# Router fed with unnormed rows, weight loads and bias products re-ordered, and the overflow table built between two item loops

## The chip, the cores and the metric

The kernel runs on one core of one Trainium2 chip. The metric is device time in microseconds (us). Five engines work side by side and meet at semaphores: TensorE (PE, matmuls), VectorE (DVE), ScalarE (ACT), GpSimd (POOL) and SyncE (SP, which here only issues transfers). Each runs its own list of instructions strictly in order.

## The reference, cut to what matters

One layer on 512 rows of 1024 values: a mixing block (gated linear attention and stick-breaking attention), a cross attention over 256 memory rows, and a mixture of experts, all in float32. The change touches only the last part.

```
h = rmsnorm(x, g_ffn)                       # x * rsqrt(mean(x*x)+eps) * g
logits = h @ w_router + b_router            # 32 experts
top 4 of 32 per row, gates = softmax(top values)
for each expert e, its rows in blocks:
    gu = xb @ w_gu[e] + b_gu[e]             # gate half, lin half (1024 each)
    act = (clip(lin)+1) * gate*sigmoid(1.702*gate)
    y = act @ w_down[e] + b_down[e]         # weighted by the gate, added to the row
y = rmsnorm(x + moe)
```

## The kernel before

The expert part works through **items**. An item is up to 96 rows of one expert, with the 8 MB of `w_gu` and 4 MB of `w_down` of that expert. Items 0 to 31 are the first 96 rows of each expert; further items would hold rows past 96 (**overflow**). The input here has none: 32 items run. Each item's weights come in 12 loads of 1 MiB ("chunks" 0 to 3 of `lin`, `gate` and `down`), issued by SP in a fixed order; a chunk's place in `ring` is loaded again once PE has multiplied it. `lin` and `down` weights are split on the chip: ACT makes the rounded part (`w_hi_a`, `w_hi_x`), DVE the remainder (`ring_split`), and PE multiplies three products.

PE's work on item t stands in two functions. `lin_and_gate(t)` multiplies the `lin` chunks (L1026) interleaved with the first half of the gate (L1007); `down_and_gate(t)` multiplies `down` (L1051) with the second half of the gate. In the steady loop PE alternates `down_and_gate(t)` and `lin_and_gate(t + 1)`. Item 0 and the start of item 1 are written out ahead of the loop, since they differ: item 0's second gate half (32 blocks) runs alone.

Ahead of the items stands the **router**, in the order that the list `ROUTE` gives PE: `y2` (the last eight pieces of the cross attention's output projection, L625), `h3` (transposes of a tile of 128 rows), `lg` (logits), `rk` (ranks of the picks within their expert), `tb` (the item table: which row stands in which slot). DVE takes the results in an order of its own (`choose`, `rank`, `weigh`, `sum_gates`); ACT norms the rows. POOL then gathers an item's 96 rows from `rows_scratch` in HBM (L2219) and later adds the results to `acc_scratch` with a scatter. `acc_scratch` starts as x plus the gated sum of `b_down`: eight **bias products** (`bd`, L981) whose results DVE adds to `X` (L1971), which is then stored.

`overflow()` on DVE (L1915 to L1956) counts further items, publishes their number (`s_items`), and prepares the overflow table. PE multiplies that in 16 matmuls (L1082), and `overflow_out()` copies it out. All of this stands between item 0 and item 1.

```
lin_transpose(0)
pe.wait_ge(s_xnext, 2)
pe.wait_ge(s_over, 1)
for n in range(16):
    last = mm(psum[0:C, Y0, 0:3 * MORE], lhsT=over_slot[:, n, :], ...)
lin_and_gate(1)
```

Of the kernel before, what the change touches and what calls it, by code (L numbers as in the profile page):

```python
# [33 lines left out]
P = 128  # L34
# [18 lines left out]
PADS = C  # L53
LIMIT = 7.0
# [5 lines left out]
class Banks:  # L60
# [41 lines left out]
]  # L102


def plan_banks():
# [48 lines left out]
    plan.add(("count",), "dve", pool=most)  # L154
    plan.add(("gatesT",), "dve", pool=most)
    for i in range(TT):
        for half in range(2):
            plan.add(("bd", i, half), "dve", pool=most)
# [8 lines left out]
def build(nc, x, mem, g_mix, w_in, w_gla_gate, b_gla_gate, g_gla_head, w_out, g_mem_q, g_mem_kv,  # L167
# [5 lines left out]
    with ExitStack() as ctx:  # L173
# [98 lines left out]
        gate_eT = VGb[:, 768:896]  # L272
        bdown = VSb[:, 1024:2048]

        MORE = MAX_ITEMS - E
        earlier_e = VGb[:, 1024:2048].rearrange("p (a b) -> p a b", a=E)
# [10 lines left out]
        oh_over = VSb[:, 0:512].rearrange("p (n e) -> p n e", n=16)  # L287
# [253 lines left out]
        def _(sp):  # L541
# [25 lines left out]
            for c in range(4):  # L567
                wait_filled(sp, SLOT_FREED[2 + c // 2])
                load_gate(0, c)
            for c in range(4):  # L570
                wait_filled(sp, SLOT_FREED[c // 2])
                load_down(0, c)
            for c in range(4):
                sp.wait_ge(s_lused, c + 1)
                load_lin(1, c)
            for c in range(4):
# [31 lines left out]
        def _(pe):  # L608
# [310 lines left out]
            def route_transpose(i):  # L919
                pe.wait_ge(s_xn, 2 * TT + i + 1)  # L920
                for u in range(2):
                    b = begin(("h3", i, u))
                    for k in range(4):
                        last = nc.tensor.transpose(b[:, k * P:(k + 1) * P],
                                                   xn[:, i, (4 * u + k) * P:(4 * u + k + 1) * P], ident[:, :])
# [21 lines left out]
            def route_table(i):  # L947
                b = begin(("table",)) if i == 0 else bank(("table",))
                pe.wait_ge(s_onehot, i + 1)
                for k in range(K):  # L950
                    last = mm(b[0:C, 0:3 * E], lhsT=in_slot[i][:, k, :], rhs=pick_rhs[:, K * i + k, :],
                              start=i == 0 and k == 0, stop=i == TT - 1 and k == K - 1)
                if i == TT - 1:
                    done(last)

# [17 lines left out]
            pe.wait_ge(s_gatee, TT)  # L973
            b = begin(("gatesT",))
            done(nc.tensor.transpose(b[:, 0:P], gate_e.rearrange("p i e -> p (i e)"), ident[:, :]))
            wait_emptied(pe, ("gatesT",))
            pe.wait_ge(s_bd, 64)
            for i in range(TT):
                for half in range(2):
                    b = begin(("bd", i, half))  # L980
                    done(mm(b, lhsT=gate_eT[i * E:(i + 1) * E, :],  # L981
                            rhs=bdown[i * E:(i + 1) * E, half * 512:(half + 1) * 512],
                            start=True, stop=True))

            wait_emptied(pe, ("bd", 3, 1))
# [11 lines left out]
            def lin_transpose(t):  # L997
# [13 lines left out]
            def lin_and_gate(t):  # L1011


                pe.wait_ge(s_xlo, t + 1)
# [3 lines left out]
                for c in range(4):  # L1018
                    pe.wait_ge(s_llo, 4 * t + c + 1)
                    for pos in range(12):  # L1020
# [4 lines left out]
                        cols_ = (lin_lo(c) if b else chunk_hi(c))[:, k2, half * 512:half * 512 + 512]  # L1025
# [9 lines left out]
                    if c == 2 and isinstance(t, int) and t == 0:  # L1035
# [23 lines left out]
            def down_and_gate(t, transpose_next=True):  # L1059
# [3 lines left out]
                for c in range(4):  # L1063
                    down_chunk(t, c, True)
                    if c == 0:
                        lin_transpose(t)
# [4 lines left out]
            pe.sem_inc(s_dused, 4)  # L1071
            item_transpose(0)
            lin_and_gate(0)
            for c in range(4):
# [5 lines left out]
            pe.wait_ge(s_over, 1)  # L1080
# [1204 lines left out]
```

## Time and profile before

| | |
|---|---|
| median of 3 runs | 1723.5 us (1723.45 to 1723.79) |
| the profiled execution, its own time | 1721.68 us |
| its span in the trace | 1719.9 us |
| PE busy | 1646.6 us, 96% |
| DVE, ACT, POOL busy | 63%, 48%, 8% |
| items, from 585.0 us on | 31 periods of about 36.1 us |

The profiled execution lies 1.8 us below the median and its span another 1.8 us below its own time. Times below are places in the span. "idle before" is the time that an engine stood still ahead of an instruction, with what ended it.

### The profile page before, as it was taken

How to read it: one execution, taken by the hardware profiler on the slowest of the kernel's cores; microseconds unless marked ns; L12 is line 12 of the kernel's file. 1: busy time of each engine (PE TensorE's matmuls, PEld its weight loads, DVE VectorE, ACT ScalarE, POOL GpSimd, SP SyncE). 2: the span in 40 equal slices, each digit the busy share in tenths (PEclk: the TensorE clock that was granted, in tenths of full speed). 3: DMA queues.
4: the chain of work that ended last, by engine and by line, in shares of the span. 5: the costliest groups of instructions: out<-in, count | busy, mean ns of one | idle time of the engine just before them, and what ended most of it. 6: DMA issues, size and time to landing. Idle time of an engine off the chain costs nothing.

```text
span 1719.9 us, 26975 instructions
## 1 busy us (share of the span) xinstructions
PE 1646.6 (96%) x10074; PEld 1380.3 (80%) x10074; DVE 1080.7 (63%) x1173; ACT 831.6 (48%) x844; POOL 132.3 (8%) x217
## 2 busy tenths in 40 slices
PE   7999989999988899999999999999999999999994
PEld 5876657987776788888888888888888888888883
DVE  4221554433357777777777777776777767777774
ACT  4243363533322446555555555555454554546553
POOL 0020220000000001000000000010000100001000
PEclk9999989999988999999999999999999999999997
DMA  5111123322049799999999999999999999999993
GB/s 204 49 50 50 49 99 122 124 89 99 16 143 396 259 375 366 377 362 374 362 382 364 376 365 363 378 375 370 368 361 382 368 370 373 362 374 370 377 338 116
DMA packets 134870, 477.09 MB, mean 277 GB/s; under 512 B 10337, under 2 KB 10386, under 8 KB 134802
## 3 DMA queue, kind: packets, MB, share of 16 engines
q1 hardware_dynamic: 123968, 446.72, 69.4%
q0 software_dynamic: 7168, 25.17, 6.2%
q10 hardware_dynamic: 3698, 4.70, 0.8%
q8 instruction: 25, 0.41, 0.1%
q14 instruction: 11, 0.09, 0.0%
HBM read 457.69 MB, written 18.87 MB: 277 GB/s over the span
## 4 chain that ended last, share of the span: by engine, by line
PE 90%; DVE 4%; ACT 3%; DMA 2%; issue 1%; ACTq 0%; POOL 0%; SPq 0%; DVEq 0%; POOLq 0%
PE psum L1007 22%; PE psum L1051 21%; PE psum L1026 20%; PE psum L625 17%; PE psum L804 1%; PE psum L793 1%; PE psum L1001 1%; PE psum L993 1%; PE psum L781 1%; PE psum L896 1%; PE psum L916 1%; DMA acc_scratch<-X 1%; ACT ring_split L1151 1%; DVE ring_split L1996 1%; PE psum L935 1%
## 5 line engine op out<-in xcount | busy, mean ns | idle before, releaser
L1007 PEld LDWEIGHTS psum<-MIX,ring 128*128 128x128 f32 x4096 | 776.1, 191 | 101.7 <-DVE MIX L2035 1.6
L1007 PE MATMUL psum<-MIX,ring 128*128 128x96 f32 x4096 | 726.5, 260 | 0.9 <-DVE MIX L2035 0.9
L1996 DVE TENSOR_TENSOR ring_split<-ring,w_hi_a 128x2048 fp32r<-128x2048 f32 x64 | 146.4, 2288 | 86.8 <-ACT w_hi_a L1417 86.4
L1026 PE MATMUL psum<-ring_split,xs_hi 128*96 128x512 f32 x512 | 200.3, 437 | 0.0
L1051 PE MATMUL psum<-ring_split,act_hi 128*96 128x512 f32 x512 | 198.1, 434 | 0.0
L2008 DVE TENSOR_TENSOR ring_split<-ring,w_hi_x 128x2048 fp32r<-128x2048 f32 x62 | 141.8, 2287 | 84.8 <-ACT w_hi_x L1428 84.8
L1996 DVE TENSOR_TENSOR ring_split<-ring,w_hi_x 128x2048 fp32r<-128x2048 f32 x64 | 146.4, 2289 | 77.5 <-ACT w_hi_x L1417 77.5
L625 PE MATMUL psum<-ring_split,H_hi 128*128 128x512 f32 (+1 forms) x512 | 151.8, 380 | 0.6 <-DVE ring L1646 0.6
L2008 DVE TENSOR_TENSOR ring_split<-ring,w_hi_a 128x2048 fp32r<-128x2048 f32 x62 | 141.6, 2284 | 2.2 <-ACT w_hi_a L1428 2.2
L1417 ACT ACTIVATE w_hi_x<-ring 128x2048 fp32r<-128x2048 f32 x64 | 121.3, 1897 | 7.3 <-DMA acc_scratch<-X 7.3
L1417 ACT ACTIVATE w_hi_a<-ring 128x2048 fp32r<-128x2048 f32 x62 | 117.7, 1899 | 12.6 <-DMA ring<-in_w_gu 12.6
L1439 ACT ACTIVATE MIX<-MIX 128x384 f32<-128x384 f32 x64 | 33.1, 517 | 182.0 <-DVE MIX L2052 182.0
L1428 ACT ACTIVATE w_hi_a<-ring 128x2048 fp32r<-128x2048 f32 x62 | 118.0, 1903 | 3.4 <-PE psum L1026 3.4
L1026 PE MATMUL psum<-w_hi_a,xs_hi 128*96 128x512 f32 x256 | 110.9, 445 | 8.0 <-DVE xs_lo L2029 8.0
L1445 ACT ACTIVATE xs_hi<-MIX 128x768 fp32r<-128x768 f32 x32 | 27.0, 845 | 188.3 <-DVE MIX L2023 188.3
L1428 ACT ACTIVATE w_hi_x<-ring 128x2048 fp32r<-128x2048 f32 x62 | 118.0, 1904 | 0.0
L1051 PE MATMUL psum<-w_hi_a,act_hi 128*96 128x512 f32 x256 | 110.0, 443 | 0.0
L1051 PE MATMUL psum<-w_hi_x,act_hi 128*96 128x512 f32 x256 | 109.5, 442 | 0.0
L1026 PE MATMUL psum<-w_hi_x,xs_hi 128*96 128x512 f32 x256 | 109.4, 439 | 0.0
L625 PEld LDWEIGHTS psum<-ring_split,H_hi 128*128 128x128 f32 x512 | 93.0, 188 | 19.1 <-DVE ring L1646 0.8
L1434 ACT ACTIVATE H<-psum 96x1024 f32<-96x1024 f32 x32 | 32.6, 1019 | 138.3 <-PE psum L1026 138.3
L1026 PE MATMUL psum<-w_hi_a,xs_lo 128*96 128x512 f32 x256 | 97.0, 425 | 0.0
(305 smaller groups left out, 2674.8 us busy)
## 6 DMA issues: line engine op xcount, KB each, us to landing
ring<-in_w_gu SPq DMA_DIRECT2D x256, 1024.0 KB, 10.3
ring<-in_w_down SPq DMA_DIRECT2D x128, 1024.0 KB, 12.1
ring<-in_w_in SPq DMA_DIRECT2D x6, 2048.0 KB, 10.1
X<-in_x SPq DMA_DIRECT2D x8, 512.0 KB, 7.6
ring<-in_w_out SPq DMA_DIRECT2D x2, 2048.0 KB, 7.8
ring<-in_w_mk SPq DMA_DIRECT2D x2, 2048.0 KB, 9.1
ring<-in_w_mv SPq DMA_DIRECT2D x2, 2048.0 KB, 7.8
ring<-in_w_mq SPq DMA_DIRECT2D x2, 2048.0 KB, 8.7
```

What stands on the lines that cost most here:

```text
L625: ins = mm(dst, lhsT=lhs(a, k), rhs=rhs(b, k), start=n == 0 and j == 0, stop=n == KT - 1 and j == 2)
L781: last = mm(sb_seg(h, i), lhsT=ksT[r:r + 64, j, i * P:(i + 1) * P], rhs=qsT[r:r + 64, j, i * P:T], start=SB_SEG[i][1] == 0, stop=True, ski ...
L1007: return mm(psum[:, dst, q * C:(q + 1) * C], lhsT=gate_w(k // 2)[:, k % 2, f * P:(f + 1) * P], rhs=xsT[:, k, :], start=k == 0 and q == 0, ...
L1026: x_last = mm(psum[0:C, L0 + half, :], lhsT=rows_, rhs=cols_, start=k == 0 and n == 0, stop=k == KT - 1 and n == 2, skip_group_check=True)
L1051: x_last = mm(psum[0:C, to + half, :], lhsT=rows_, rhs=cols_, start=f == 0 and n == 0, stop=f == KT - 1 and n == 2, skip_group_check=True)
L1417: go(chunk_hi(c), lin_w(c), ACT.Copy).then_inc(s_lhi, 1)
L1428: go(chunk_hi(c), down_w(c), ACT.Copy).then_inc(s_dhi, 1)
L1434: go(lin_rows.rearrange("p (a b) -> p a b", a=2), psum[0:C, 2:4, :], ACT.Copy)\
L1439: go(sig_h, gate_h, ACT.Sigmoid, scale=ALPHA).then_inc(s_sig, 1)
L1445: go(xs_hi[:, :, :], xs_next, ACT.Copy).then_inc(s_xhi, 1)
L1996: v.tensor_tensor(lin_lo(c), lin_w(c), chunk_hi(c).bitcast(F32), ALU.subtract)\
L2008: v.tensor_tensor(down_lo(c), down_w(c), chunk_hi(c).bitcast(F32), ALU.subtract)\
```

## The change

- **Router.** PE transposes `X` itself and not the normed rows; the scale `rstd` is applied to the logits when DVE takes them. ACT computes `rstd` first (`rstd_3`) and the normed rows after it (`rows_3`). `ROUTE` and DVE's order are changed.
- **Table.** The item table holds rows only; its gates come from 16 matmuls of their own (`route_gates`, bank `tgate`), after the counts.
- **Loads.** Item 0's `lin` chunks are issued ahead of the row stores, and two of its `gate` chunks ahead of the last of these. `down` chunks 2 and 3 of item 0 wait for the first gather; 0 and 1 stand behind `lin` chunks 2 and 3 of item 1, since their place now holds the rounded part of item 0's `lin` chunks 2 and 3 (`first_hi`). The stores to `acc_scratch` go from ACT's queue to SP's, between `lin` chunks 1 and 2 of item 1.
- **Bias products.** Five of eight stand ahead of `lin_and_gate(0)`, three inside it. `item_transpose(0)` no longer waits for them.
- **Overflow.** `overflow()` keeps the count of items, with a shorter running sum. The rest is `overflow_rows()`; it, PE's 16 matmuls and `overflow_out()` stand behind the item loop's passes 1 and 2. The loop is now two loops, 1 to 2 and 3 to m. POOL gathers items 1 to 5 before it waits for the table.

```diff
+            for i in range(TT):
+                if i == TT - 1:
+                    for c in range(2):
+                        wait_filled(sp, SLOT_FREED[2 + c // 2])
+                        load_gate(0, c)
...
+                sp.wait_ge(s_xn, 2 * TT + i + 1)
+                sp.dma_start(rows_dram[i * P:(i + 1) * P, :], xn[:, i, :]).then_inc(s_rowsout, 16)
...
             def route_transpose(i):
-                pe.wait_ge(s_xn, 2 * TT + i + 1)
+                pe.wait_ge(s_res, TT + i + 1)
...
-            wait_emptied(pe, ("bd", 3, 1))
...
+            wait_emptied(pe, ("tgate",))
             item_transpose(0)
+            wait_emptied(pe, ("gatesT",))
+            pe.wait_ge(s_bd, 64)
+            for piece in BD[0:3]:
+                add_bias(piece)
+            pe.wait_ge(s_xnext, 1)
+            for piece in BD[3:5]:
+                add_bias(piece)
             lin_and_gate(0)
...
-            with pe.Fori(1, m) as t:
+            with pe.Fori(1, TABLE_AT) as t:
+                down_and_gate(t, after_table=False)
+                lin_and_gate(t + 1)
+            pe.wait_ge(s_over, 1)
+            for n in range(16):
+                last = mm(psum[0:C, T0, 0:3 * MORE], lhsT=over_slot[:, n, :], rhs=over_rhs[:, n, :],
+                          start=n == 0, stop=n == 15)
+            last.then_inc(s_overt, 1)
+            with pe.Fori(TABLE_AT, m) as t:
                 down_and_gate(t)
                 lin_and_gate(t + 1)
...
+            with dve.Fori(1, TABLE_AT) as t:
+                item(t)
+            overflow_rows()
+            overflow_out()
+            with dve.Fori(TABLE_AT, m) as t:
+                item(t)
```

SP's list, from the row stores to item 1's gate loads, before (L556 is `load_lin`, L559 `load_gate`, L562 `load_down`):

```order
L554 DMA rows_scratch<-A 128x1024 [waits normed_rows_ready] x4
L556 DMA ring<-in_w_gu 128x2x1024 [waits psum_bank_filled] x4
L559 DMA ring<-in_w_gu 128x2x1024 [waits psum_bank_filled] x4
L562 DMA ring<-in_w_down 128x2x1024 [waits psum_bank_filled] x4
L556 DMA ring<-in_w_gu 128x2x1024 [waits lin_chunk_multiplied] x4
L559 DMA ring<-in_w_gu 128x2x1024 [waits gate_chunk_multiplied] x4
```

The same stretch after the change (L565 is `load_lin`, L568 `load_gate`, L571 `load_down`):

```order
L565 DMA ring<-in_w_gu 128x2x1024 [waits psum_bank_filled] x4
L585 DMA rows_scratch<-A 128x1024 [waits normed_rows_ready] x3
L568 DMA ring<-in_w_gu 128x2x1024 [waits psum_bank_filled] x2
...
L585 DMA rows_scratch<-A 128x1024 [waits normed_rows_ready]
L568 DMA ring<-in_w_gu 128x2x1024 [waits psum_bank_filled] x2
...
L565 DMA ring<-in_w_gu 128x2x1024 [waits lin_chunk_multiplied] x2
L598 DMA acc_scratch<-X 128x1024 [waits residual_with_bias_ready] x4
L565 DMA ring<-in_w_gu 128x2x1024 [waits lin_chunk_multiplied]
L571 DMA ring<-in_w_down 128x2x1024
L565 DMA ring<-in_w_gu 128x2x1024 [waits lin_chunk_multiplied]
L571 DMA ring<-in_w_down 128x2x1024
L568 DMA ring<-in_w_gu 128x2x1024 [waits gate_chunk_multiplied] x4
```

Four stores and two `down` loads now stand between item 1's `lin` loads, and all of them ahead of its `gate` loads.

PE's list around the overflow table after the change (the last rows of the first loop, the 16 matmuls, the head of the second loop):

```order
L1062 MATMUL psum<-w_hi_x,xs_lo 96x512 x2
L1132 REGISTER_ALU
L1132 COMPARE_AND_BRANCH
L1137 MATMUL psum<-MIX,RGb 96x63 [waits overflow_onehots_ready]
L1137 MATMUL psum<-MIX,RGb 96x63 x15
L1140 UNCONDITIONAL_BRANCH
L1140 ISA
L1082 ISA [waits gate_half_clamped]
L1084 REGISTER_ALU [waits down_chunk_lo_ready]
L1091 MATMUL psum<-w_hi_a,act_hi 96x512 [waits act_half_lo_ready]
```

Before, the 16 matmuls (L1082) stood right behind `lin_transpose(0)` and ahead of `lin_and_gate(1)`.

DVE's list at the same place after the change (the end of an item's pass, then `overflow_rows`):

```order
L2077 TENSOR_TENSOR ring_split<-ring,w_hi_a 128x2048 [waits down_chunk_hi_ready]
L2204 REGISTER_ALU
L2204 COMPARE_AND_BRANCH
L1997 TENSOR_SCALAR QGb<-QGb 128x16
L1999 SCALAR_TENSOR_TENSOR QGb<-QGb 128x16 [waits dve_step] x4
...
L2019 TENSOR_TENSOR RGb<-KDb,QGb 128x1536
L1947 TENSOR_SCALAR KDb<-psum,QGb 96x21 [waits overflow_table_filled]
```

The vector work that PE's 16 matmuls wait for now begins only after DVE's last instruction of the pass for item 2.

## Rows read from the trace of the kernel before

**Rows 1.** The page: span, and the chain that ended last.

```profile
span 1719.9 us, 26975 instructions
PE 90%; DVE 4%; ACT 3%; DMA 2%; issue 1%; ACTq 0%; POOL 0%; SPq 0%; DVEq 0%; POOLq 0%
```

**Rows 2.** Windows: start:end, length, busy by engine, granted PE clock, DMA share, GB/s.

```profile
512.00:519.00 7.00, 5.14 (x17) 1.94 (x17) 2.86 (x11) 1.63 (x1) 1.14 (x1) 0.54 1.04 400
529.00:533.00 4.00, 4.00 (x16) 3.52 (x16) 2.25 (x2) 0.00 (x0) 0.00 (x0) 0.50 1.03 411
533.00:556.00 23.00, 23.00 (x171) 20.74 (x169) 18.31 (x42) 8.55 (x6) 0.92 (x1) 1.00 1.03 397
564.00:571.00 7.00, 6.14 (x25) 5.16 (x24) 6.52 (x14) 2.85 (x3) 0.00 (x0) 0.53 0.38 152
571.00:585.00 14.00, 14.00 (x91) 11.86 (x91) 8.26 (x9) 4.24 (x3) 0.00 (x0) 1.00 0.64 200
585.00:621.00 36.00, 36.00 (x241) 31.04 (x240) 26.56 (x26) 19.39 (x16) 2.71 (x3) 1.00 0.99 338
```

**Rows 3.** Timeline of PE, router to item 0: start, length, idle before.

```profile
502.33 3.56 PE L935 MATMUL psum<-QGb,RGb 128*128 128x32 f32 x16 [0.71 <-DVE RGb L1803]
...
514.33 4.92 PE L981 MATMUL psum<-VSb,VGb 32*128 32x512 f32 x16 [0.38 <-DVE VGb L1911]
523.30 1.51 PE L993 MATMUL psum<-ident,H 96*128 96x96 f32 x8 [4.05 <-DVE X L1971]
528.63 0.74 PE L1026 MATMUL psum<-w_hi_a,xs_hi 128*96 128x512 f32 x1 [3.82 <-DVE xs_lo L2029]
```

**Rows 4.** Timeline of DVE: router, head of item 0.

```profile
501.50 0.68 DVE L1803 COPY RGb<-psum 128x512 f32<-128x512 f32 x1
...
523.48 2.29 DVE L1996 TENSOR_TENSOR ring_split<-ring,w_hi_a 128x2048 fp32r<-128x2048 f32 x1 [0.33 <-DVE X L1971]
525.69 1.02 DVE L2023 TENSOR_TENSOR MIX<-psum,gcols 128x384 f32<-128x384 f32 x2
```

**Rows 5.** POOL's gathers: issue of the first, and its time to landing.

```profile
513.45 1.14 POOL L2219 DMA_INDIRECT H<-rows_scratch,KDb  x1 [58.73 <-DVEq L1904]
...
DMA to landing us min/median/max: 8.4/8.4/8.4
```

**Rows 6.** Timeline of PE, items 0 to 2.

```profile
539.52 0.40 PE L1026 MATMUL psum<-w_hi_x,xs_hi 128*96 128x512 f32 x1
...
548.87 7.28 PE L1007 MATMUL psum<-MIX,ring 128*128 128x96 f32 x64
555.98 0.85 PE L1001 MATMUL psum<-ident,H 96*128 96x96 f32 x8
556.67 2.85 PE L1082 MATMUL psum<-MIX,RGb 128*96 128x63 f32 x32
563.70 0.67 PE L1026 MATMUL psum<-w_hi_a,xs_hi 128*96 128x512 f32 x1 [4.18 <-DVE xs_lo L2029]
565.23 0.74 PE L1007 MATMUL psum<-MIX,ring 128*128 128x96 f32 x2 [0.86 <-DVE MIX L2035]
...
576.30 0.40 PE L1026 MATMUL psum<-w_hi_x,xs_hi 128*96 128x512 f32 x1
...
585.00 0.40 PE L1051 MATMUL psum<-w_hi_a,act_hi 128*96 128x512 f32 x1
...
621.11 0.40 PE L1051 MATMUL psum<-w_hi_a,act_hi 128*96 128x512 f32 x1
```

**Rows 7.** DMA issues from 571 to 586 us: size, us from issue to landing.

```profile
ring<-in_w_gu SPq DMA_DIRECT2D x4, 1024.0 KB, 5.4
```

**Rows 8.** Timeline of DVE: the overflow work, and the end of an item's pass.

```profile
548.03 0.17 DVE L1934 TENSOR_SCALAR QGb<-QGb 128x16 f32<-128x16 f32 x1
...
552.97 1.75 DVE L1956 TENSOR_TENSOR RGb<-KDb,QGb 128x1536 f32<-128x1536 f32 x1
...
617.14 2.28 DVE L2008 TENSOR_TENSOR ring_split<-ring,w_hi_a 128x2048 fp32r<-128x2048 f32 x1
```

More of the change, by code:

```diff
@@ L53 @@
 PADS = C
+TABLE_AT = 3
 LIMIT = 7.0
@@ L98 @@
 ROUTE = [
[3 rows of a table removed]
-]
[3 rows of a table added]
+]
+BD = [(i, half) for half in range(2) for i in range(TT)]
+BD_BANK = dict(zip(BD, (1, 6, 7, 4, 5, 1, 4, 5)))
 def plan_banks():
@@ L153, in plan_banks @@
     plan.add(("table",), "dve", pool=(7,))
[L154 to L158, printed above, removed]
+    plan.add(("count",), "dve", pool=(0,))
+    plan.add(("tgate",), "dve", pool=(3,))
+    plan.add(("gatesT",), "dve", pool=(2,))
+    for i, half in BD:
+        plan.add(("bd", i, half), "dve", pool=(BD_BANK[i, half],))
     return plan
@@ L954, in route_table, with route_gates @@
                     done(last)
+            def route_gates():
+                b = begin(("tgate",))
+                for i in range(TT):
+                    pe.wait_ge(s_gatee, i + 1)
+                    for k in range(K):
+                        last = mm(b[0:C, 0:E], lhsT=in_slot[i][:, k, :], rhs=pick_rhs[:, K * i + k, 2 * E:3 * E],
+                                  start=i == 0 and k == 0, stop=i == TT - 1 and k == K - 1)
+                done(last)
             for step in ROUTE:
@@ L972, in _, with add_bias @@
             done(mm(b[:, 0:E], lhsT=ones[:, :], rhs=picks_upto[:, TT - 1, :], start=True, stop=True))
-            pe.wait_ge(s_gatee, TT)
+            route_gates()
             b = begin(("gatesT",))
             done(nc.tensor.transpose(b[:, 0:P], gate_e.rearrange("p i e -> p (i e)"), ident[:, :]))
[L976 to L983, printed above, removed]
-            wait_emptied(pe, ("bd", 3, 1))
+            def add_bias(piece):
+                i, half = piece
+                b = begin(("bd", i, half))
+                done(mm(b, lhsT=gate_eT[i * E:(i + 1) * E, :],
+                        rhs=bdown[i * E:(i + 1) * E, half * 512:(half + 1) * 512], start=True, stop=True))
             G0, G1, L0, T0, Y0 = 0, 1, 2, 4, 6
@@ L1011, in lin_and_gate @@
             def lin_and_gate(t):
+                first = isinstance(t, int) and t == 0
                 pe.wait_ge(s_xlo, t + 1)
@@ L1079, in _ @@
             pe.wait_ge(s_xnext, 2)
-            pe.wait_ge(s_over, 1)
-            for n in range(16):
-                last = mm(psum[0:C, Y0, 0:3 * MORE], lhsT=over_slot[:, n, :], rhs=over_rhs[:, n, :],
-                          start=n == 0, stop=n == 15)
-            last.then_inc(s_overt, 1)
             lin_and_gate(1)
@@ L1873, in _ @@
             sum_gates(0)
+            add_residual("y2", 2, 1)
+            choose(1)
+            rank(0)
             add_residual("y2", 3, 0)
             h3_out(2)
-            choose(1)
-            rank(0)
             weigh(1)
@@ L2080, in _ @@
             xT_next(0)
+            add_bias(BD[0])
             xT_lo(0)
@@ L2107, in _, with item @@
             st.finish()
-            with dve.Fori(1, m) as t:
+            def item(t):
                 st = Steps(t)
```

206 lines of the change are left out of this document (121 added, 85 removed), and 6 rows, old and new, of the table ROUTE.

## The prediction, made before the result was known

> **What bounds the kernel now.** I read the page first: 90% of the chain that ended last is PE [rows 1]. So time is won only where PE stands still, runs at the lower clock, or does work that can go. The windows by stage say where that is. From 585 us on PE is busy in all of the stretch at a granted clock of 1.00 [rows 2], and an item takes 621.11 - 585.00 = 36.1 us of PE work [rows 6]. Both kernels run the same 31 such periods, so the comparison is settled by the moment at which `down_and_gate(1)` starts (585.0 before), plus whatever is put in behind it. PE's timeline ahead of that shows the waits: 4.05 us and 3.82 us around the first item's transposes [rows 3], and 4.18 us and 0.86 us ahead of item 1 [rows 6]. The windows add the clock: 0.50 to 0.54 (the lower of its two levels, 1.2 of 2.4 GHz) from 512 to 533 and again from 564 to 571 [rows 2]. Last I read the transfers: from 512 to 564 they run without a break at 397 to 411 GB/s [rows 2].
>
> **Router.** It should save nothing. PE transposes the last tile earlier, since it no longer waits for the normed rows. But the logits' matmuls began at 502.33, released by DVE's copy at 501.50 [rows 3, 4], and in DVE's new order that copy still stands behind `choose(2)` and `rank(1)`. What is won is small: `rk` of the last tile stands ahead of one `tb`, and the gates leave the table. I put the first gather's issue 0.5 us earlier, from 513.45 to 513.0 [rows 5].
>
> **Item 0 starts earlier.** Before, the gather landed 8.4 us after its issue [rows 5] with the transfers at 400 GB/s [rows 2], and PE then waited for the bias sums until 523.30 [rows 3]. After, `lin` and most `gate` loads are over and the `down` loads wait for the gather, so it meets idle engines. Its 0.39 MB (96 rows of 4 KB) at 400 GB/s take 1 us; no row shows an unloaded gather. I estimate 6.4 us (bounds 5.5 and 8.4), so 519.4. Transposes at the lower clock take 1.5 us [rows 3]: 520.9. From `xT_next` to the first matmul took 528.63 - 525.69 = 2.94 us [rows 3, 4], and the one bias sum put between fits ScalarE's time there. Start: **523.8** (522.3 to 525.8) against 528.63, 4.8 us won. The matmuls for `tgate` (32 passes, half of them ahead of the last gates) and DVE's first 2.29 us subtraction fill the wait for the gather; if they come last instead, they cost up to the upper bound.
>
> **Item 0 itself.** From its start to the end of chunk 1 was 539.52 - 528.63 = 10.9 us, while two chunks take 585.00 - 576.30 = 8.7 us at full clock [rows 6], so the lower clock cost 2.2. PE is busier ahead of item 0 now, so I charge half of that: chunk 1 ends at 523.8 + 8.7 + 1.1 = 533.6 (531.0 to 536.7). Three bias products inside the item add about 0.9 us (eight took 4.92 at the lower clock [rows 3], 0.31 each at full). The item to the end of `lin_transpose(0)` was 556.67 - 528.63 = 28.0 us [rows 3, 6]; now 28.0 + 0.9 - 1.1 = 27.8, ending at 551.6. Were nothing else in the way, PE would begin item 1 there.
>
> **What is late next: item 1's gate weights.** A gate chunk's place is free only when item 0's separate second gate half has used it, so this load cannot be early. SP's new list puts ahead of it, all issued from the end of chunk 1 on: `lin` 1, four stores (2 MiB), `lin` 2, `down` 0, `lin` 3, `down` 1. With the gate chunk that is 8 MiB; `g_final`'s 0.5 MiB and one gather (0.4) share the engines: 8.9 MiB. The last issue before it comes less than 11 us after the first, so the queue never drains. At the 405 GB/s of the windows [rows 2] a MiB takes 2.6 us. A single load met idle engines in 5.4 us [rows 7]. So `gate` 0 lands at 533.6 + 5.4 + 7.9 x 2.6 = **559.5**, and PE, which after its first matmul needs it at 551.9, stands for 7.6 us. Bounds: 24 us (8.9 MiB at the highest rate shown, 411 GB/s, and little more than a start of a microsecond) to 26.5 us after the end of chunk 1, so 555.0 to 563.2. The other three gate chunks follow at 2.6 us and PE uses one in 4.35, so they do not delay it.
>
> The Trainium skill, "DMA: Bandwidth & Descriptors", section Bandwidth, gives about 358 GB/s as what HBM grants one core and lets that side bind loads. By that a MiB takes 2.93 us and PE would wait 2.9 us longer. The windows here stand at 397 to 411 for 50 us, so the measurement decides, and the page's figure is left a small chance.
>
> **Item 1.** Before, from 563.70 to 585.00 = 21.3 us: 17.4 at full clock (twice 8.7), 0.86 of waiting, 3.0 for the clock, which was 0.53 behind 4.18 us of standing still [rows 2, 6]. After 7.6 us of standing still it will be low again. A stretch at the lower clock cost 2.2 and 3.0 us in these two places; I take 2.6 (1.8 to 3.4). `down_and_gate(1)` starts at 559.5 + 17.1 + 2.6 = **579.2**, against 585.0: 5.8 us won.
>
> **The table is now paid for.** Before, DVE's overflow work (548.03 to 554.72 = 6.7 us [rows 8]) lay under item 0's gate blocks, and PE's 2.85 us of matmuls lay in a gap that ended at 563.70 anyway [rows 6]: together they cost nothing. After, `overflow_rows` starts when DVE ends its pass, at 617.14 + 2.28 = 619.4 in a period that PE ends at 621.1 [rows 6, 8], 1.7 us ahead of PE. It takes 6.7 us, so PE stands 5.0 us. Then come the 2.85 us of matmuls, and the lower clock again, since 4.18 us of standing still were enough for it: 2.6. Sum **10.4 us** (9.6 to 11.3). DVE has slack in the next item (26.6 busy of 36 [rows 2]) and `overflow_out` (six instructions on at most 96 x 21 values) lies under `down` chunk 0, so nothing further is late. POOL's wait for the table stands behind five gathers and holds up nothing.
>
> **Sum.** -5.8 + 10.4 = +4.6 us. The profiled execution would go from 1721.7 to 1726.3 us of its own time; the median is 1.8 above that, so **1728.1 us**. At the bounds: start 522.3, chunk 1 at full clock, 24 us and 1.8 give 573.9, and with 9.6 a sum of -1.5; the other end gives 583.7 and with 11.3 a sum of +10.0.
>
> **Rivals.**
> - *The gate chunk is there in time* (faster). Place: PE's second instruction of item 1. PE would start item 1 at 551.6, keep the full clock, and reach `down_and_gate(1)` at 569.0: 16.0 won, 10.4 paid, **-5.6 us, 1717.9**. For it: loads are issued so early that the queue stands empty before the end of chunk 1. Against: 8.9 MiB need over 22 us at the rate of any window shown, and PE leaves 18. It decides the sign once gate 0 lands before about 555. Chance 0.15.
> - *DVE's table work is hidden*. If DVE ran ahead of PE by 7 us in passes 1 and 2, only 2.85 us would be paid: -3.0 us, **1720.5**. For it: DVE is idle 9 us in each item [rows 2]. Against: that idle time lies inside the pass, in waits for ScalarE and PE; its last instruction ends 1.7 us ahead of PE [rows 6, 8]. Chance 0.12.
> - *Item 0 is no earlier*. If gate matmuls, the subtraction and the gather's fixed time come one after another, the start stays at 528.6 and all behind it moves 4.8 us: +9.4, **1732.9**. Against: the 4.05 us wait for the bias sums is surely gone [rows 3]. Chance 0.12.
> - *The slower transfer rate*: +7.5, **1731.0**. Chance 0.05.
> - That the router part does nothing is already in the sum; were it to bring the logits forward by the 3 us of the norming, the result would be 1725.
>
> **How the numbers follow.** A difference of 0.2% (3.4 us) is about what a measurement of this kernel can tell from no change. The forecast has 0.56, with a range of its own of 1722 to 1733; some 0.7 of it lies above 1727. Slower: 0.56 x 0.7 + 0.12 + 0.05, less a little for what I overlook on the good side, 0.53. Faster: the first rival and a part of the second, 0.18. Within 0.2%: 0.29. The range goes from the first rival to the third, 1718 to 1733.
>
> **What would show it.** Right: in the changed trace PE's first matmul of item 0 near 523.8; a PE wait of 6 to 9 us at the first gate matmul of item 1, ended by a load of `w_gu`, with a clock near 0.5 behind it; one wait of about 5 us ahead of the 16 table matmuls two periods later, ended by DVE's `over_slot`, again with the lower clock; then periods of 36.1 us to the end. Wrong: no wait for that load; DVE done with the table when PE comes; a clock that stays at 1.00 over either wait (2.6 us less each); or a first matmul later than 526.

## The result and the profile after

The changed kernel is slower: 1730.35 us median of 5 runs (1729.2 to 1732.91) against 1723.5 us of before (1723.04 to 1723.86) on the same chip. The recorded ratio of the runs is 1.0046, with a 95% interval of 1.0035 to 1.0058 (the quotient of the two medians is 1.0040). The profiled execution took 1730.79 us of its own time.

The page of the changed kernel, its span, its chain and its costliest group:

```profile
span 1729.0 us, 27040 instructions
...
PE 91%; ACT 3%; DVE 3%; DMA 2%; issue 1%; ACTq 0%; POOL 0%; SPq 0%; DVEq 0%; POOLq 0%
...
L1041 PE MATMUL psum<-MIX,ring 128*128 128x96 f32 x4096 | 727.1, 260 | 10.1 <-DMA ring<-in_w_gu 10.1
```

The chain reads like that of before [rows 1], though PE's gate matmuls now have 10.1 us of idle time ahead of them, all for one load. PE's waits in the changed kernel, from the router to item 4 (engine, line, releaser: us in total, times, longest us):

```profile
PE psum L1041 <- DMA ring<-in_w_gu: 10.1, 1, 10.1
PE psum L1137 <- DVE RGb L2019: 4.8, 1, 4.8
PE psum L962 <- DVE RGb L1856: 1.9, 1, 1.9
PE psum L1025 <- DMA H<-rows_scratch,KDb: 0.6, 1, 0.6
```

The waits around item 0 are gone (4.05 and 3.82 us in [rows 3]). Two have come: 10.1 us for item 1's gate weights and 4.8 us for the overflow table. The windows of the changed kernel (columns as in [rows 2]):

```profile
512.00:519.00 7.00, 6.40 (x40) 6.13 (x39) 3.95 (x17) 5.21 (x3) 1.14 (x1) 0.50 0.27 78
529.00:533.00 4.00, 4.00 (x27) 3.39 (x26) 3.84 (x3) 0.00 (x0) 0.00 (x0) 1.00 0.23 51
...
535.00:537.00 2.00, 2.00 (x13) 1.08 (x13) 0.69 (x1) 0.00 (x0) 0.00 (x0) 1.00 0.63 143
537.00:545.00 8.00, 8.00 (x59) 7.02 (x58) 6.65 (x25) 3.83 (x2) 0.92 (x1) 1.00 0.99 351
545.00:556.00 11.00, 8.78 (x77) 8.27 (x75) 8.18 (x10) 4.19 (x4) 0.00 (x0) 1.00 1.03 368
556.00:564.00 8.00, 0.11 (x1) 0.14 (x1) 7.27 (x10) 2.85 (x3) 0.00 (x0) 0.50 1.02 412
564.00:571.00 7.00, 7.00 (x28) 6.00 (x29) 1.82 (x3) 0.00 (x0) 0.00 (x0) 0.60 0.80 320
...
630.00:666.00 36.00, 31.17 (x201) 27.13 (x200) 25.03 (x36) 17.15 (x14) 2.74 (x3) 0.89 0.91 337
666.00:690.00 24.00, 24.00 (x158) 20.82 (x158) 18.38 (x24) 9.00 (x7) 1.13 (x2) 0.95 0.73 220
```

In the first two of these windows, around item 0's start, the transfers nearly rest now (78 and 51 GB/s, where [rows 2] have 400 and 411). From 556 to 564 the queues are full, at 412 GB/s, while PE does nothing and its clock falls to the lower level. PE's own rows in the changed kernel:

```profile
504.15 3.01 PE L962 MATMUL psum<-QGb,RGb 128*128 128x32 f32 x16 [1.86 <-DVE RGb L1856]
...
518.86 1.51 PE L1025 MATMUL psum<-ident,H 96*128 96x96 f32 x8 [0.60 <-DMA H<-rows_scratch,KDb]
520.30 3.77 PE L1016 MATMUL psum<-H,STb 32*128 32x512 f32 x10
524.01 0.74 PE L1062 MATMUL psum<-w_hi_a,xs_hi 128*96 128x512 f32 x1
...
563.89 0.71 PE L1041 MATMUL psum<-MIX,ring 128*128 128x96 f32 x2 [10.12 <-DMA ring<-in_w_gu]
...
583.81 0.40 PE L1091 MATMUL psum<-w_hi_a,act_hi 128*96 128x512 f32 x1
...
661.02 5.38 PE L1137 MATMUL psum<-MIX,RGb 128*96 128x63 f32 x32 [4.83 <-DVE RGb L2019]
666.16 0.72 PE L1091 MATMUL psum<-w_hi_a,act_hi 128*96 128x512 f32 x1
```

Item 0 starts at 524.01 (before 528.63), item 1's gate at 563.89, `down_and_gate(1)` at 583.81 (before 585.00 [rows 6]). The last row but one is the table: PE stood 4.83 us, and its matmuls took 5.38 us instead of 2.85 [rows 6].

**Where the difference arose.** Work ahead of the router's last matmuls takes a different time in each execution, by up to 5 us. So I cut each trace in two: from the start of the logits of tile 2 (the "anchor": 496.23 before, 497.99 after) to `down_and_gate(1)`, and from there to the end of the span.

| kernel | anchor to `down_and_gate(1)` | from there to the end |
|---|---|---|
| before | 88.8 | 1134.9 |
| changed | 85.8 | 1145.2 |
| changed, a second trace | 84.1 | 1146.3 |

The head won 3.0 us (4.7 in the second trace), the rest lost 10.3 (11.4).

### The profile page after: what moved, and what is told of

The parts are those of the page before. It is cut to its first block, busy times and chain, and to the rows that moved or that the text cites. A ratio compares the mean times of both kernels' runs of the same rounds, so it can differ in the third digit from the quotient of the medians.

```text
span 1729.0 us, 27040 instructions
## 1 busy us (share of the span) xinstructions
PE 1656.2 (96%) x10106; PEld 1389.4 (80%) x10106; DVE 1079.8 (62%) x1178; ACT 831.5 (48%) x844; POOL 129.3 (7%) x213
## 4 chain that ended last, share of the span: by engine, by line
PE 91%; ACT 3%; DVE 3%; DMA 2%; issue 1%; ACTq 0%; POOL 0%; SPq 0%; DVEq 0%; POOLq 0%
PE psum L1041 23%; PE psum L1091 21%; PE psum L1062 20%; PE psum L652 17%; PE psum L831 1%; PE psum L1025 1%; PE psum L820 1%; PE psum L1035 1%; PE psum L808 1%; DMA ring<-in_w_gu 1%; PE psum L923 1%; PE psum L943 1%; ACT ring_split L1203 1%; PE psum L962 0%; DVE ring_split L1613 0%
## 5 line engine op out<-in xcount | busy, mean ns | idle before, releaser
L1041 PEld LDWEIGHTS psum<-MIX,ring 128*128 128x128 f32 x4096 | 777.1, 191 | 110.9 <-issue 10.4
L1041 PE MATMUL psum<-MIX,ring 128*128 128x96 f32 x4096 | 727.1, 260 | 10.1 <-DMA ring<-in_w_gu 10.1
L2077 DVE TENSOR_TENSOR ring_split<-ring,w_hi_x 128x2048 fp32r<-128x2048 f32 x62 | 141.8, 2288 | 82.1 <-ACT w_hi_x L1481 82.1
L2065 DVE TENSOR_TENSOR ring_split<-ring,w_hi_x 128x2048 fp32r<-128x2048 f32 x62 | 141.9, 2289 | 71.8 <-ACT w_hi_x L1470 71.8
L1470 ACT ACTIVATE w_hi_x<-ring 128x2048 fp32r<-128x2048 f32 x62 | 117.6, 1897 | 3.7 <-DMA ring<-in_w_gu 3.7
L1481 ACT ACTIVATE w_hi_x<-ring 128x2048 fp32r<-128x2048 f32 x62 | 118.0, 1903 | 0.0
L1062 PE MATMUL psum<-w_hi_x,xs_hi 128*96 128x512 f32 x248 | 105.9, 439 | 0.0
```

The lines of the kernel that those rows point to most:

```text
L1041: return mm(psum[:, dst, q * C:(q + 1) * C], lhsT=gate_w(k // 2)[:, k % 2, f * P:(f + 1) * P], rhs=xsT[:, k, :], start=k == 0 and q == 0, ...
L1062: x_last = mm(psum[0:C, L0 + half, :], lhsT=rows_, rhs=cols_, start=k == 0 and n == 0, stop=k == KT - 1 and n == 2, skip_group_check=True)
L1470: go(chunk_hi(c), lin_w(c), ACT.Copy).then_inc(s_lhi, 1)
L1481: go(chunk_hi(c), down_w(c), ACT.Copy).then_inc(s_dhi, 1)
L2065: v.tensor_tensor(lin_lo(c), lin_w(c), hi.bitcast(F32), ALU.subtract)\
L2077: v.tensor_tensor(down_lo(c), down_w(c), chunk_hi(c).bitcast(F32), ALU.subtract)\
```

## The experiments

The first four ran on one chip (before there: 1721.24 us), the next four on a second (1722.61), the last three on a third (1722.16). Ratios are to the runs of before on the same chip.

**1. The table back between items 0 and 1.** The first loop runs from 1 to m again, on PE and DVE; all else stays as changed.

```diff
             pe.wait_ge(s_xnext, 2)
+            pe.wait_ge(s_over, 1)
+            for n in range(16):
+                last = mm(psum[0:C, Y0, 0:3 * MORE], lhsT=over_slot[:, n, :], ...)
             lin_and_gate(1)
```

> The changed kernel with one thing undone: the overflow rows, the 16 table matmuls and the copy out stand between items 0 and 1 again, and the item loop is one loop. Theory (two new waits): in the changed kernel the table costs 11.3 us (4.8 us of PE standing still, 5.4 us of matmuls at the lower clock, the rest the lower clock behind them), and here it falls into PE's 10.1 us wait for item 1's gate weights, so it costs nothing: about 1719 us against 1730.4 for the changed kernel and 1723.5 for before. Rival 1 (the table costs its matmuls only, the loss lies elsewhere): 1727.5 us. Rival 2 (the overflow work delays item 1's rows on VectorE past the landing of the gate weights): 1721 us or more, with a PE wait on xs_lo or on the one-hots ahead of item 1.

Measured: 1719.39 us, ratio 0.9991 (0.998 to 1.0002). PE in this kernel, around the table:

```profile
556.21 4.29 PE L1131 MATMUL psum<-MIX,RGb 128*96 128x63 f32 x32 [1.46 <-DVE RGb L2016]
...
564.58 0.71 PE L1041 MATMUL psum<-MIX,ring 128*128 128x96 f32 x2 [3.60 <-DMA ring<-in_w_gu]
```

The wait for the gate chunk is 3.6 us where it was 10.1, though the chunk lands at the same distance from the anchor (65.5 us; 65.9 in the changed kernel). The table work lies in time in which PE would have stood anyway. The rest behind `down_and_gate(1)` is 1134.6 us, as before. So the whole loss, and more, is the table's. A little of rival 2 is there, a wait of 1.46 us for the one-hots, but it lies ahead of a gate chunk that PE would have waited for anyway.

**2. Item 1's gate chunks ahead of item 0's `down` chunks 0 and 1**, the table still behind item 2.

```diff
             for c in range(2, 4):
                 sp.wait_ge(s_lused, c + 1)
                 load_lin(1, c)
-                load_down(0, c - 2)
             for c in range(4):
                 sp.wait_ge(s_gused, c + 1)
                 load_gate(1, c)
+            for c in range(2):
+                load_down(0, c)
```

> The changed kernel with SP's list altered in one place: item 0's down chunks 0 and 1 are issued behind item 1's four gate loads instead of ahead of them. Theory (PE waits for gate chunk 0 because 8.9 MiB stand ahead of it in the queue): 2 MiB less ahead of it, so it lands 5 us earlier, PE's wait of 10.1 us shrinks to about 5, and the time is about 1725.3 us. Rival 1 (the wait has another cause than the queue, such as the issue time): still 10 us, 1730.4 us. Rival 2 (the two down chunks are then late for item 1): a new PE wait ahead of the down products, 1728 us or more.

Measured: 1725.44 us, ratio 1.0023 (1.0014 to 1.0033). PE's first gate matmul of item 1 in this kernel:

```profile
557.59 0.71 PE L1042 MATMUL psum<-MIX,ring 128*128 128x96 f32 x2 [4.95 <-DMA ring<-in_w_gu]
```

That is 60.7 us behind the anchor, 5.2 us earlier than in the changed kernel (65.9 and 65.4 in its two traces, 66.5 in experiment 7, which is the same up to there): about what two loads of 1 MiB take at 2.6 us. PE's wait halves, and `down_and_gate(1)` comes 5.9 us sooner than in the first trace of the changed kernel and 4.2 sooner than in the second.

**3. `overflow_rows()` on DVE during item 0**, with only `overflow_out()` and PE's matmuls left between the loops.

```diff
             lin_lo_part(1, 0)
+            overflow_rows()
...
-            overflow_rows()
             overflow_out()
             with dve.Fori(TABLE_AT, m) as t:
```

> The changed kernel with VectorE's overflow_rows (6.7 us) moved back between items 0 and 1; PE's 16 matmuls and the copy out stay behind item 2, between the two loops. Theory (the table is dear because PE stands still for VectorE and the clock falls): no PE wait ahead of the 16 matmuls, they run at the full clock in 2.9 us, and the table costs 3 us in place of 11.3: about 1722 us. Rival (the narrow matmuls themselves or the loop's border bring the clock down, or cost the time): 5.4 us of matmuls at the lower clock again, 1726 us or more.

Measured: 1722.74 us, ratio 1.001 (1.0 to 1.002). PE's table matmuls in this kernel have no wait and run at full clock:

```profile
659.08 2.85 PE L1137 MATMUL psum<-MIX,RGb 128*96 128x63 f32 x32
```

The rest behind `down_and_gate(1)` is 1137.2 us, 2.3 above before, against 10.3 above in the changed kernel. So 8.0 us hang on the wait, of which it is itself only 4.8.

**4. PE's transpose of the router waits for the normed rows again**, and ACT writes those first.

```diff
-                pe.wait_ge(s_res, TT + i + 1)
+                pe.wait_ge(s_xn, 2 * TT + i + 1)
```

> The changed kernel, but PE's router transposes wait for the normed rows as before (the rows that they read stay the unnormed ones; ScalarE norms the last tile ahead of its copy). Theory (the last tile's logits wait for VectorE's copy, which stands behind choose(2) and rank(1), not for the transposes): no difference, 1730.4 us within 1 us. Rival (unnormed rows bring the logits forward by the norming): 2 to 3 us slower than the changed kernel, about 1733 us.

Measured: 1731.32 us, ratio 1.0063 (1.0049 to 1.0077), on another chip than the pair of the result. PE's transposes of the last tile in this kernel:

```profile
499.99 1.97 PE L951 MATMUL psum<-ident,X 128*128 128x128 f32 x8 [1.61 <-ACT A L1427]
```

The recorded theory (no difference, since DVE's copy holds the logits) fell in its place: the wait is back, and the last tile's logits start 7.7 us behind the anchor, 6.2 in the changed kernel and 6.1 before. Item 0 starts 2.2 us later in the trace, and since PE then waits for the same gate chunk, `down_and_gate(1)` comes only 0.8 us later. So the unnormed rows do carry 1.6 to 2 us in the new order, and the new order of the stages takes as much away: the router as a whole delivers its logits no sooner than before.

**5. Edits 1 and 2 together.**

> The two repairs of e1 and e2 together: the table between items 0 and 1, and item 0's down chunks 0 and 1 behind item 1's gate loads. Theory: in e1 PE ended the table's matmuls 61.4 us behind the start of the last logits-but-one and waited 3.6 us more for gate chunk 0; in e2 that chunk landed 60.7 us behind the same point. So no wait for it is left, PE starts item 1 when the table's matmuls end, and the kernel is 3 to 4.5 us faster than e1: a ratio of about 0.9970 to before (1718.5 us against 1723.5). Rival (VectorE's chain is next, since the table now delays the rows of item 1 and lin chunk 1 of item 1): equal to e1 within 1 us, with PE waits on xs_lo or on ring_split inside item 1.

Measured: 1712.99 us, ratio 0.9945 (0.9931 to 0.9959). It beats both kernels. PE's waits in it, from 506 to 800 us:

```profile
PE psum L1132 <- DVE RGb L2017: 1.5, 1, 1.5
PE psum L1026 <- DMA H<-rows_scratch,KDb: 0.6, 1, 0.6
PE psum L973 <- DVE QGb L1876: 0.2, 1, 0.2
```

More was won than the expected 0.9970. Against the changed kernel the table below accounts for most of it: the head is 4.7 us shorter (80.3 against a mean of 85.0) and the rest 11.4, together 16.1 of the 17.9 us between the medians of this chip. Against experiment 1 the heads differ by 3.8 us, as expected; the ratios differ by more (0.9991 for experiment 1, on another chip), and no trace shows why. There is no wait for a weight any more. The table's 1.5 us of waiting and 4.3 us of matmuls lie where PE stood 4.95 us in experiment 2, so they are all but free there (the head is 80.3 against 79.9), and nothing is left to pay behind `down_and_gate(1)` (1134.7 us). The clock still falls, after only 1.5 us of standing still:

```profile
556.00:571.00 15.00, 15.00 (x91) 13.40 (x91) 13.94 (x23) 6.82 (x6) 0.00 (x0) 0.77 1.03 412
```

PE is busy in all of these 15 us at 0.77 of the clock: at most 3.4 us of time still lie here.

**6. Before, with only the table moved** (behind item 2, two loops, POOL's gathers 1 to 5 first); loads, router and bias products as before.

```diff
-            with pe.Fori(1, m) as t:
+            with pe.Fori(1, TABLE_AT) as t:
+                down_and_gate(t, after_table=False)
+                lin_and_gate(t + 1)
+            pe.wait_ge(s_over, 1)
...
+            with pe.Fori(TABLE_AT, m) as t:
```

> The kernel before with one part of the change alone: the overflow rows, the 16 matmuls and the copy out behind item 2, between two loops (the old count, router, loads and bias products stay). Theory: the table costs 11.3 us there, and 3 to 4.5 us come back since VectorE has item 1's rows ready 6.7 us sooner and PE then waits for the gate chunk: 7 to 8.5 us slower than before, a ratio of 1.0045. Rival 1 (the table's place costs nothing, it was the other parts): ratio 1.000 or below. Rival 2 (nothing comes back): 11.3 us, a ratio of 1.0065.

Measured: 1730.91 us, ratio 1.005 (1.0036 to 1.0063). PE in this kernel:

```profile
563.56 0.71 PE L1030 MATMUL psum<-w_hi_a,xs_hi 128*96 128x512 f32 x1 [4.15 <-DVE xs_lo L2039]
...
661.68 5.24 PE L1092 MATMUL psum<-MIX,RGb 128*96 128x63 f32 x32 [4.82 <-DVE RGb L1966]
```

The cost shows without the rest of the change: the same 4.8 us wait, the same slow matmuls, and 1145.6 us behind `down_and_gate(1)`. The total is as expected (8.3 us by the medians), but what came back is 2.8 us for the 3 to 4.5 expected, and not for the reason given: PE waits for `xs_lo`, not for the gate chunk. From item 0's first matmul to item 1's is 32.3 us (563.56 - 531.29), where it was 35.1 before (563.70 - 528.63). So the table work between items 0 and 1 cost before 2.8 us. The rows of DVE show whose: first those of before, then those of this kernel.

```profile
555.57 4.48 DVE L1996 TENSOR_TENSOR ring_split<-ring,w_hi_a 128x2048 fp32r<-128x2048 f32 x2
562.69 0.96 DVE L2029 TENSOR_TENSOR xs_lo<-MIX,xs_hi 128x768 fp32r<-128x768 f32 x1
...
553.39 2.29 DVE L2006 TENSOR_TENSOR ring_split<-ring,w_hi_a 128x2048 fp32r<-128x2048 f32 x1 [1.09 <-ACT w_hi_a L1424]
557.58 2.29 DVE L2006 TENSOR_TENSOR ring_split<-ring,w_hi_a 128x2048 fp32r<-128x2048 f32 x1 [1.90 <-ACT w_hi_a L1424]
562.50 0.96 DVE L2039 TENSOR_TENSOR xs_lo<-MIX,xs_hi 128x768 fp32r<-128x768 f32 x1
```

Before, DVE comes from the overflow rows and works without a gap up to `xs_lo`. Here it stands still for ScalarE's rounding, and its second subtraction (the remainder of `lin` 1) ends 28.6 us behind item 0's first matmul (559.87 - 531.29) where it ended after 31.4 (560.05 - 528.63); `xs_lo` follows 3.6 us later in both. So the 2.8 us are DVE's. PE's 2.85 us of matmuls, nearly the same number, ended at 559.5, 4.18 us ahead of `xs_lo`, and lay inside the wait.

**7. The table one item earlier** (`TABLE_AT = 2`).

```diff
-TABLE_AT = 3
+TABLE_AT = 2
```

> The changed kernel with the border between the two loops behind item 1 in place of item 2 (one number). Theory: VectorE ends every pass 1.7 us ahead of PE, so the table costs the same 11 us wherever in the items it stands: equal to the changed kernel within 1.5 us, with a PE wait of 4.8 us ahead of the 16 matmuls one period earlier. Rival (behind item 1 VectorE is further behind or ahead of PE, since item 1 began with the long wait for its gate weights): a PE wait of a different length, and 3 us or more of difference.

Measured: 1732.13 us, ratio 1.0056 (1.0042 to 1.007). PE around the table in this kernel:

```profile
623.76 5.38 PE L1137 MATMUL psum<-MIX,RGb 128*96 128x63 f32 x32 [4.83 <-DVE RGb L2019]
```

The same wait to the hundredth, one period earlier. The cost belongs to DVE's place behind its pass, not to the particular item.

**8. The changed kernel once more**, unaltered, beside the last three.

> The changed kernel once more, unaltered, on the chip of this group, for its spread and for a second profile. Expected: a ratio of 1.0046 within 0.001; from the last row of the cross attention's output to the start of item 0 26.0 us, PE's wait for gate chunk 0 of item 1 10.1 us, for the one-hots 4.8 us; what differs from the first profile lies ahead of that, in code that the change does not touch.

Measured: 1730.94 us, ratio 1.005 (1.0036 to 1.0064). The waits in its trace are 9.7 us and 4.8 us at the same two lines, and item 0 starts 25.6 us behind the anchor.

**9. The four stores behind item 1's gate chunk 0** instead of between its `lin` chunks 1 and 2.

```diff
-            for i in range(TT):
-                sp.wait_ge(s_x2b, i + 1)
-                sp.dma_start(acc_dram[i * P:(i + 1) * P, :], X[:, i, :])...
...
             for c in range(4):
                 sp.wait_ge(s_gused, c + 1)
                 load_gate(1, c)
+                if c == 0:
+                    for i in range(TT):
+                        sp.wait_ge(s_x2b, i + 1)
+                        sp.dma_start(acc_dram[i * P:(i + 1) * P, :], X[:, i, :])...
```

> The changed kernel with the four stores to acc_scratch behind item 1's gate chunk 0 instead of between its lin chunks 1 and 2. In the changed kernel that gate chunk landed 28.7 us after the issue of lin chunk 1 (563.9 - 535.2). If the whole stretch simply runs at one lower rate (8.9 MiB in 28.7 us less 5.4 is 2.95 us per MiB), taking 2 MiB out brings the chunk 5.9 us forward, to 22.8 us. If the transfers run at 405 GB/s but for the stores, which leave the engines partly idle and slow, it comes forward by 7 to 8 us and is then held by the issues alone (lin 2 at 5.5 us, 5 MiB from there: 21.4 us), and the window behind the stores' old place stands at 395 to 411 GB/s instead of 368. ScalarE waits for the stores ahead of its third rounding of item 1's lin chunks, so PE will stand still there instead, in both theories: the span says nothing, the landing does.

One run, 1729.9 us. PE's first gate matmul of item 1 came 63.4 us behind the anchor, 2.5 us earlier than in the changed kernel's first trace and 2.0 earlier than in its second. Its row, and then the windows of the same kernel:

```profile
561.13 0.71 PE L1042 MATMUL psum<-MIX,ring 128*128 128x96 f32 x2 [7.66 <-DMA ring<-in_w_gu]
```

```profile
537.00:545.00 8.00, 8.00 (x57) 6.98 (x56) 6.71 (x26) 3.33 (x2) 0.92 (x1) 1.00 0.84 258
545.00:556.00 11.00, 8.47 (x75) 8.05 (x73) 8.20 (x11) 2.28 (x3) 0.00 (x0) 1.00 1.01 349
```

Both expectations fell. In this one trace the stores cost the chunk 2 to 2.5 us, less than the 5.9 of an even rate and far less than 7 to 8. Without them the stretch runs slower, 258 GB/s where it was 351, since SP waits for PE to free the next `lin` place and the engines have little queued. And the later stretch stands at 349, not at 395 or more: the stores are not what keeps the rate below 400 there.

**10. Edits 2 and 3 together**, the table's matmuls still behind item 2, and **11. experiment 5 again** on the same chip.

> The changed kernel with both remedies that leave the table at the third item: item 1's gate chunks issued ahead of item 0's down chunks 0 and 1, and overflow_rows on DVE during item 0. Theory (wait of PE for each, additive): the table then costs 2.5 us of matmuls alone as in the kernel with early rows, and the rest behind down_and_gate(1) is 1137.2 us; down_and_gate(1) starts 80 to 81 us behind the anchor unless DVE, now with 6.7 us more work under item 0, releases item 1's low part late (it did so in the kernel with early rows, by 3.4 us, which lay under the longer wait for the gate chunk). With that wait in the open: 82 us, a time 4.5 us below before, ratio 0.9975. Rival: the table's place does not matter once DVE is ahead, and this kernel equals the one with the table back at item 1 and the gates first (0.9945).

> The kernel with the table back between items 0 and 1 and the gate chunks first, unaltered, beside the previous one on the same chip: 0.993 to 0.996 again if its gain is real.

Measured: 1716.74 us, ratio 0.9972 (0.9962 to 0.9983), and 1713.46 us, ratio 0.9956 (0.9943 to 0.997). PE's waits in the first of the two, from 506 us on:

```profile
PE psum L1063 <- DVE xs_lo L2099: 3.3, 1, 3.3
PE psum L1042 <- DMA ring<-in_w_gu: 0.8, 1, 0.8
```

The wait for item 1's low part is in the open, as expected, since DVE's 6.7 us of table work now lie ahead of it. The rest is 1137.7 us against 1134.0 in the other: the 16 matmuls alone cost about 3 us where PE would not have stood still, also with DVE ahead. The rival is refuted: the eight runs of the first kernel (1715.11 to 1717.78) and the five of the second (1712.51 to 1715.11) meet only at their ends. Of the places tried, the table is cheapest between items 0 and 1.

All traces in one table (us):

| kernel | anchor to `down_and_gate(1)` | from there to the end |
|---|---|---|
| before | 88.8 | 1134.9 |
| 6 only the table moved | 86.0 | 1145.6 |
| changed; again; 7; 9 | 85.8; 84.1; 86.1; 84.1 | 1145.2; 1146.3; 1146.9; 1146.3 |
| 4 waits for normed rows | 86.6 | 1146.1 |
| 1 table back | 84.1 | 1134.6 |
| 2 gates first | 79.9 | 1145.7 |
| 3 rows early | 85.9 | 1137.2 |
| 10 gates first, rows early | 79.8 | 1137.7 |
| 5 and 11, gates first, table back | 80.3; 80.3 | 1134.7; 1134.0 |

The head of one and the same kernel differs by 2 us between traces. The sum of both columns also doesn't give the medians exactly: experiment 1 should be 4.9 us below before by it and its median is 1.9 below; over all eleven the medians lie some 1.1 us higher on average. Whether that is the part ahead of the anchor or this one trace of before stays open. The right column, which carries the verdict, has three levels and nothing between: table in the gap (mean of four 1134.6), table late with its rows early (1137.5), table late (mean of seven 1146.0).

## Why the prediction was right, and where it was off

The forecast was 1728.1 us (+4.6) and the result 1730.35 (+6.85). The direction and the mechanism held. The term of the head was mis-sized (a gain of 5.8 us, where the two traces show 3.0 and 4.7), the term of the table was right to a microsecond, and one statement on the kernel before was wrong without touching the sum.

- **Router saves nothing: right on the whole.** The last logits began 6.2 us behind the anchor, 6.1 before. My reason was incomplete: experiment 4 shows that without the removed wait they would have been 1.6 us later in the new order.
- **Item 0 starts earlier: right, and by more than forecast.** It started 26.0 us behind the anchor where it was 32.4: 6.4 us won for 4.8 forecast. That 524.01 meets the forecast place of 523.8 is luck, since all of this trace stands 1.8 us later (anchor 497.99 for 496.23). The gather was issued 16.4 us behind the anchor (514.43), 17.2 before: 0.8 us earlier for 0.5. Its rows were used at 518.86, 4.4 us after the issue, where I had 6.4 with 5.5 as the lower bound. Then the bias products, which I had put beside ScalarE's work, filled the time to 524 (3.77 us).
- **Chunk 1's end:** `lin` 1 of item 1, which waits for it and is the second of two in the first row of SP's list below, was issued at 535.2, 11.2 us after item 0's start, for 9.8 forecast. I had charged half of one clock loss of 2.2 us; it was a whole one and a little more.
- **The wait for item 1's gate chunk: right in place and cause, mis-sized.** "So `gate` 0 lands at 559.5 and PE stands for 7.6 us": it was 563.9 and 10.1 us.

  Of the 4.4 us between the landings, 1.6 are chunk 1's end; the other 2.8 are the transfers, which took 28.7 us from there for 25.9 (26.5 was my upper bound). The mis-sized step is "so the queue never drains" with 8.9 MiB and 405 GB/s.

  First the rate: the windows show 143, 351 and 368 GB/s in 2, 8 and 11 us; against 405 these lack 0.52, 0.43 and 0.41 MB, which is 3.4 us. My 5.4 us for the first load had 2.8 in hand for that (2.6 of the 5.4 are its bytes). Then the bytes: from the issue of `lin` 1 to the landing of `gate` 0, [535.2, 563.9], the queues moved 10.32 MB, and 8.9 MiB are 9.33. Of the 1.0 MB more, 0.1 are the rest of `lin` 0, and nearly all of what is left can only be of the gate chunks behind `gate` 0, the only other loads in SP's queue. At 405 the 1.0 MB are 2.4 us. So 25.9 + 2.4 + 3.4 - 2.8 = 28.9 us, for 28.7 measured. The view of [535.2, 563.9]:

```profile
DMA packets 2725, 10.32 MB, mean 360 GB/s; under 512 B 213, under 2 KB 213, under 8 KB 2722
```

  SP's list in the same trace:

```profile
530.84 4.71 SPq L565 DMA_DIRECT2D ring<-in_w_gu  x2
535.59 3.42 SPq L598 DMA_DIRECT2D acc_scratch<-X  x4
540.77 0.38 SPq L565 DMA_DIRECT2D ring<-in_w_gu  x1
541.20 1.07 SPq L571 DMA_DIRECT2D ring<-in_w_down  x1
...
547.55 7.50 SPq L568 DMA_DIRECT2D ring<-in_w_gu  x4
```

  A load issued at 535.2 meets engines that have all but finished the one before (DMA share 0.63 in [535, 537]), so they idle until it arrives. Between 545 and 556 the share is 1.03 and the rate still 368 (397 in the same place before [rows 2]). The lack is not spread evenly:

```profile
545.00:547.50 2.50, 2.50 (x22) 2.31 (x21) 2.48 (x3) 1.70 (x2) 0.00 (x0) 1.00 1.04 411
547.50:551.50 4.00, 4.00 (x39) 4.00 (x37) 2.61 (x5) 0.57 (x2) 0.00 (x0) 1.00 1.04 295
551.50:556.00 4.50, 2.28 (x22) 1.96 (x20) 3.09 (x3) 1.91 (x1) 0.00 (x0) 1.00 1.01 408
```

  All of it lies in four microseconds, in which a gather is in flight (issued by POOL at 541.68, landed 9.7 us later). Before, the same dip stands at 549.5 to 552.5 (309 GB/s), with the gather issued at 544.96 and landed after 7.7. In twelve of the thirteen traces such a dip begins 4 to 7 us after that gather's issue (in experiment 9 the rate was low already and came back as the gather landed), and it comes later where the gather does (experiment 3: issue at 544.70, 277 GB/s in [551, 554]). Experiment 9 excludes the stores as the reason. No run leaves the gather out, so it is the likely cause and not a shown one.
- **The rival of the slower transfer rate.** The stretch behaved on average as that rival says: 360 GB/s over its 28.7 us. The Trainium skill, "DMA: Bandwidth & Descriptors", section Bandwidth, has about 358 GB/s per core as what binds a load; the same section gives it as the share of each core when both of a pair stream, and here one core runs. The agreement is not a confirmation: the windows stand at 412 GB/s right behind, from 556 to 564, and moving 2 MiB away in experiment 2 gave 2.6 us for each MiB, the price at 405. The average is low because of the stretch that is not full and the dip above. (My +7.5 for this rival charged 2.9 us; 7.9 MiB at 0.33 us more each are 2.6.)
- **Item 1: right.** 19.9 us from the landing to `down_and_gate(1)` for 19.7 forecast (17.1 + 2.6); 18.7 in the second trace. Clock after the wait 0.60 over [564, 571].
- **The table is paid for: right.** 10.3 us in the trace for 10.4 (11.4 as the mean over seven traces against four). Wait 4.83 for 5.0; the matmuls 2.85 at full clock (experiment 3) and 5.38 after the wait. The wait of 4.8 us costs 8.5 us by the three levels (1146.0 - 1137.5): 3.7 of these are the clock, above my 2.6 and above its upper bound of 3.4.
- **"Together they cost nothing"** was wrong of the kernel before: experiment 6 puts the table's place there at 2.8 us. PE's 2.85 us of matmuls did lie in the gap, as I had it. DVE's 6.7 us did not lie wholly under the gate blocks: they pushed back its second subtraction and with it `xs_lo`, for which PE waits. It did not enter the sum, since in the changed kernel the gate chunk sets item 1's start. In experiments 1 and 5 the table is indeed all but free there: their heads are no longer than those of the kernels beside them without it (84.1 among 84.1 to 86.1; 80.3 against 79.9).
- **The sum.** Forecast -5.8 and +10.4. In the trace, against the anchor, -3.0 and +10.3 give +7.3; the medians give +6.85. The head's 5.8 became 3.0 in four steps: item 0's start +1.6, chunk 1's end -1.4, the transfers -2.8, item 1 -0.2. So an error in my favour hid part of the late gate chunk.

The rivals: the gate chunk in time, and item 0 no earlier, are refuted by their rows; the hidden DVE work by the 4.83 us wait. That experiments 5 and 11 gain some 9 us on before shows where the change's own gain went: much of item 0's earlier start was given back to a gate load that SP issues behind two `down` loads, and the table cost more than all that was left.

## What to carry to other kernels

Work that lies in a gap is nearly free, and the same work between two passes of a full loop costs its length, its wait and the clock behind the wait: here 16 matmuls of 2.85 us came to 11 us. "In a gap" has to hold for both engines: before, PE's matmuls lay in PE's gap, and DVE's part still cost 2.8 us. Before moving such work, look at whose instruction order starts it: DVE reaches the end of its pass only 1.7 us ahead of PE, so all that is put there is a wait. When a stage is made to start earlier, look for the first transfer that can't be issued earlier, count what the queue has ahead of it, and move behind it whatever is needed later: exchanging six issues in SP's list was worth 4 to 6 us.

## What the runs showed of the chip

- PE's clock fell to its lower level behind a wait of only 1.5 us (experiment 5): the granted clock is 1.00 over [553, 555.65], in which the wait lies, and 0.50 from 557 to 563, though PE was busy in all of that. The 16 narrow matmuls right behind the wait already took 4.3 us instead of 2.85. The kernel before had shown it for shorter waits still, which I had overlooked: in its router 16 logits matmuls of one tile took 1.86 us at 496.23 and the 16 of the next 3.56 at 502.33 [rows 3]. Between them the longest waits were 0.88 and 0.71 us (PE was busy in 4.74 of the 6 us up to 502), and over [503, 508] the granted clock is 0.50.

```profile
496.23 1.86 PE L935 MATMUL psum<-QGb,RGb 128*128 128x32 f32 x16
...
500.16 1.09 PE L924 MATMUL psum<-ident,A 128*128 128x128 f32 x8 [0.88 <-ACT A L1374]
```

- An indirect gather of 96 rows of 4 KB was usable 4.4 us after its issue with the transfers at 78 GB/s, and landed after 8.4 us with them at 400 [rows 5].
- Busy transfer engines are not always engines at their rate: share 0.99 to 1.03 went with 349 to 368 GB/s in some stretches and 397 to 412 in others. Within [545, 556] of the changed kernel it was 1.04 with 295 GB/s for 4 us while an indirect gather was in flight.
- The first 500 us, whose work is nearly the same in all kernels, ended between 496.1 and 501.0 us in thirteen traces. A difference of less than 5 us between the spans of two single traces says nothing here until both are cut at a common point.
